# A two-layer diffusion trunk on one core: low activation halves stored backwards in one tensor with the high ones, and gate tiles that take both in one matmul of 512 columns

## What is computed

```python
h  = rms_norm(x, norm_w) * (1 + scale) + shift          # latent tokens
hc = rms_norm(ctx, norm_w) * (1 + scale_c) + shift_c    # context tokens
# SSD mixer: w_in gives z (4096), x (4096), B and C (8 groups x 128 each), dt
z, xbc, dt = jnp.split(t @ w_in, ...)
xbc = silu(conv_centred(xbc, conv_w, conv_b))           # width 5
...                                                     # chunked scans in both directions give y
y   = y * silu(z)
out = rms_norm(y, gn_w) @ w_out
```

## Time and profile before

| what | value |
|---|---|
| median of 3 runs | 2082.49 us (2082.2 to 2082.69) |
| the profiled execution, its own time | 2082.66 us |
| its span in the trace | 2081.0 us, mean granted TensorE clock 0.99 |
| TensorE busy | 2020.3 us (97% of the span), 10490 matmuls |
| TensorE weight loads | 1673.6 us (80%) |
| VectorE busy | 1459.7 us (70%) |
| ScalarE busy | 966.8 us (46%) |
| GpSimd busy | 671.5 us (32%) |
| chain that ended last | PE 80%, DVE 7%, DMA 4%, issue 3%, ACT 3%, POOL 2% |

### The profile page before, as it was taken

One profiled execution on the slowest core, in us unless ns is written; L12 is line 12 of the kernel. 1 busy time (PEld: TensorE's weight loads), 2 busy tenths in 40 slices (PEclk: granted clock), 3 DMA queues, 4 the chain that ended last, 5 costly groups with the idle time before them and its releaser, 6 DMA issues.

```text
span 2081.0 us, 31064 instructions
## 1 busy us (share of the span) xinstructions
PE 2020.3 (97%) x10490; PEld 1673.6 (80%) x10490; DVE 1459.7 (70%) x2070; ACT 966.8 (46%) x1397; POOL 671.5 (32%) x568
## 2 busy tenths in 40 slices
PE   5999999999999999999999999999999999999998
PEld 2567888888888888878878888888888888888886
DVE  5257777777777777774348887787878787877544
ACT  3244444445444444453355445445444444456443
POOL 1135666555555555635200211111112111110011
PEclk8999999999999999999999999999999999999999
DMA  9976666766666766646453554554554645456654
GB/s 352 370 218 148 165 170 176 182 173 175 165 175 172 179 175 175 165 131 174 110 151 85 153 146 127 151 136 127 150 139 123 166 116 146 132 151 197 227 184 155
DMA packets 418610, 349.23 MB, mean 168 GB/s; under 512 B 13600, under 2 KB 358272, under 8 KB 417920
## 3 DMA queue, kind: packets, MB, share of 16 engines
q1 hardware_dynamic: 393456, 273.43, 45.9%
q0 software_dynamic: 19968, 70.26, 14.1%
q10 hardware_dynamic: 5136, 4.89, 0.7%
HBM read 344.21 MB, written 4.33 MB: 167 GB/s over the span
## 4 chain that ended last, share of the span: by engine, by line
PE 80%; DVE 7%; DMA 4%; issue 3%; ACT 3%; POOL 2%; SPq 0%; DVEq 0%; POOLq 0%; ACTq 0%
PE bank L366 20%; PE bank L370 20%; PE bank L368 20%; DMA arena<-in_na_ada_w_dram 3%; PE bank L2255 3%; PE bank L2257 2%; PE bank L2256 2%; DVE w_lo L351 2%; PE bank L2193 1%; PE bank L2174 1%; DVE arena L1624 1%; PE bank L1996 1%; PE bank L1970 1%; PE bank L2188 1%; PE bank L1998 1%
## 5 line engine op out<-in xcount | busy, mean ns | idle before, releaser
L366 PE MATMUL bank<-act_hi,w_hi 128*128 128x512 f32 (+1 forms) x2448 | 906.7, 370 | 18.0 <-DVE w_lo L351 10.6
L370 PE MATMUL bank<-act_hi,w_lo 128*128 128x512 f32 (+1 forms) x2448 | 889.1, 363 | 0.0
L368 PE MATMUL bank<-act_lo,w_hi 128*128 128x512 f32 (+1 forms) x2448 | 888.8, 363 | 0.0
L351 DVE TENSOR_TENSOR w_lo<-arena,w_hi 128x2048 fp32r<-128x2048 f32 x184 | 435.6, 2368 | 210.1 <-ACT w_hi L347 147.7
L366 PEld LDWEIGHTS bank<-act_hi,w_hi 128*128 128x128 f32 x2448 | 463.0, 189 | 104.4 <-DVE w_lo L351 19.9
L370 PEld LDWEIGHTS bank<-act_hi,w_lo 128*128 128x128 f32 x2448 | 462.9, 189 | 73.7
L368 PEld LDWEIGHTS bank<-act_lo,w_hi 128*128 128x128 f32 x2448 | 463.5, 189 | 68.1
L610 POOL TENSOR_TENSOR acc<-acc,arena 128x512 f32<-128x512 f32 x224 | 330.4, 1475 | 122.9 <-ACT arena L835 113.6
L347 ACT ACTIVATE w_hi<-arena 128x2048 fp32r<-128x2048 f32 x138 | 263.8, 1911 | 85.2 <-PE bank L2257 78.2
L835 ACT ACTIVATE arena<-arena,cond_c 128x512 f32<-128x512 f32 x256 | 171.3, 720 | 264.6 <-POOL acc L610 152.5
L1392 DVE SCALAR_TENSOR_TENSOR arena<-arena,cond_c 128x512 f32<-128x512 f32 x240 | 248.4, 1035 | 65.3 <-DMA arena<-in_ssd_ada_w_dram 39.2
(11 more groups left out here) (255 smaller groups left out, 2166.0 us busy)
## 6 DMA issues: line engine op xcount, KB each, us to landing
arena<-in_ssd_w_in_dram SPq DMA_DIRECT2D x81, 1024.0 KB, 6.0
arena<-in_na_w_in_dram SPq DMA_DIRECT2D x58, 1024.0 KB, 7.4
arena<-in_ssd_ada_w_dram POOLq DMA_DIRECT2D x96, 512.0 KB, 4.1
arena<-in_na_ada_w_dram SPq DMA_DIRECT2D x64, 512.0 KB, 9.2
arena<-in_ssd_w_out_dram SPq DMA_DIRECT2D x32, 1024.0 KB, 5.1
arena<-in_na_ada_w_dram POOLq DMA_DIRECT2D x32, 512.0 KB, 4.2
arena<-in_na_w_out_dram SPq DMA_DIRECT2D x16, 1024.0 KB, 6.2
arena<-cs_scr SPq DMA_DIRECT2D x64, 256.0 KB, 5.2
```

The source lines that it names most:

```text
L351: nc.vector.tensor_tensor(w_lo[:, n0 % 2, :], raw[slot], w_hi[:, n0 % 2, :].bitcast(F32), ALU.subtract).then_inc(s_lo, 1)
L366: nc.tensor.matmul(bank[b][:, 0:cols], hi[:, w], act_hi3[:, k, 0:cols], start=(k == 0), stop=False)
L368: nc.tensor.matmul(bank[b][:, 0:cols], hi[:, w], act_lo3[:, k, 0:cols], start=False, stop=False)
L370: mm = nc.tensor.matmul(bank[b][:, 0:cols], lo[:, w], act_hi3[:, k, 0:cols], start=False, stop=(k == KT - 1))
```

## The change

`act_hi` and `act_lo` become one tensor `act` with 16 blocks of 1024 columns. In a block the low parts come first, in reverse order of the tokens, then the high parts in their own order, so that the middle 512 columns are: latent low parts backwards, latent high parts forwards. All writers and readers of `act_lo3` go through a view with step -1; `y_low` of the output projection is stored forwards, in the same places.

The G tiles use a new `project_z`. For each k it issues one matmul of 512 columns (`w_hi` by the middle 512 columns) and one of 256 (`w_lo` by the latent high parts, into the bank's second half); for the last k the 256-wide one comes first. The bank then holds the high x low part, backwards, in its first half and the rest in its second. The C tiles stay as they were.

VectorE gets `z_sum`: a copy of the first half read backwards into `silu_z`, a wait for it, and a sum with the second half into `silu_z`, which frees bank 0. ScalarE's tanh now reads `silu_z` and waits for that; it stands behind `hi_s(5 + 2j)` instead of ahead of it (in the last group it stays ahead of the second output tile's high part). VectorE's `z_gate_s` stands behind `lo_s(5 + 2j)`, reads only SBUF, and no longer frees the bank. In the last group `z_sum(3)` stands behind `y_low(0, 8)` and ahead of `fin_lo(1)`.

The diff, with lines left out that only carry context:

```diff
@@ -57,7 +57,7 @@
 OUT_BANK = (6, 0, 6, 0)
-SSD_STEPS = 54
+SSD_STEPS = 62
@@ -118,8 +118,7 @@
             pass
-        act_hi = sb("act_hi", [P, KT * TOK], F32R)
-        act_lo = sb("act_lo", [P, KT * TOK], F32R)
+        act = sb("act", [P, KT * 2 * TOK], F32R)
         w_hi = sb("w_hi", [P, 2, D], F32R)
@@ -159,12 +158,17 @@
-        act_hi3 = act_hi[:, :].rearrange("p (k t) -> p k t", k=KT)
-        act_lo3 = act_lo[:, :].rearrange("p (k t) -> p k t", k=KT)
-        def y_place(act3, k):
-            return act3[:, k, LAT:TOK] if k < KT else act3[:, k - KT, 0:LAT]
+        act3 = act[:, :].rearrange("p (k t) -> p k t", k=KT)
+        act_hi3 = act3[:, :, TOK:2 * TOK]
+        act_lo3 = act3[:, :, 0:TOK][:, :, ::-1]
+        def y_hi(k):
+            return act3[:, k, TOK + LAT:2 * TOK] if k < KT else act3[:, k - KT, TOK:TOK + LAT]
+        def y_lo(k):
+            return act3[:, k, 0:CTX] if k < KT else act3[:, k - KT, CTX:TOK]
@@ -373,6 +377,21 @@
                 mm.then_inc(s_used, 1)
+        def project_z(pe, n0, turn):
+            b = n0 % 2
+            pe.wait_ge(s_lo, turn.at(n0 + 1))
+            pe.wait_ge(s_free[b], turn.half(n0 // 2))
+            for k in range(KT):
+                w = slice(k * P, (k + 1) * P)
+                if k == KT - 1:
+                    nc.tensor.matmul(bank[b][:, LAT:TOK], w_lo[:, b, w], act_hi3[:, k, 0:LAT], start=False, stop=False)
+                mm = nc.tensor.matmul(bank[b][:, :], w_hi[:, b, w], act3[:, k, CTX:CTX + 2 * LAT],
+                                      start=(k == 0), stop=(k == KT - 1))
+                if k < KT - 1:
+                    nc.tensor.matmul(bank[b][:, LAT:TOK], w_lo[:, b, w], act_hi3[:, k, 0:LAT], start=False, stop=False)
+            mm.then_inc(s_used, 1)
@@ -1027,8 +1046,8 @@
             def z_tanh_s(j, t10):
-                act.wait_ge(s_used, t10.at(N_SSD + 3 + 2 * j + 1))
-                nc.scalar.activation(z_tanh, bank[0][:, 0:LAT], ACT.Tanh, scale=0.5).then_inc(s_zth, 1)
+                act.wait_ge(s_free[0], t10.half((N_SSD + 3 + 2 * j) // 2 + 1))
+                nc.scalar.activation(z_tanh, silu_z[j % 2], ACT.Tanh, scale=0.5).then_inc(s_zth, 1)
@@ -1070,7 +1089,7 @@
                     act.wait_ge(s_y, k + 1)
-                    nc.scalar.activation(y_place(act_hi3, k), y_t[:, k, :], ACT.Copy,
+                    nc.scalar.activation(y_hi(k), y_t[:, k, :], ACT.Copy,
                                          scale=colk[:, V_GN + k:V_GN + k + 1]).then_inc(s_yhi, 1)
@@ -1105,8 +1124,8 @@
                 else:
+                    hi_s(1, t10)
                     z_tanh_s(3, Turn(g, 10, -10))
-                    hi_s(1, t10)
                     decays(-1, t4)
@@ -1142,8 +1161,8 @@
                     if j < PAIRS - 1:
+                        hi_s(5 + 2 * j, t10)
                         z_tanh_s(j, t10)
-                        hi_s(5 + 2 * j, t10)
                         if j == 0:
@@ -1632,10 +1651,17 @@
+            def z_sum(j, t10):
+                dve.wait_ge(s_used, t10.at(N_SSD + 3 + 2 * j + 1))
+                step(nc.vector.tensor_copy(silu_z[j % 2], bank[0][:, 0:LAT][:, ::-1]))
+                step.wait()
+                nc.vector.tensor_tensor(silu_z[j % 2], silu_z[j % 2], bank[0][:, LAT:TOK], ALU.add)\
+                  .then_inc(s_free[0], 1)
             def z_gate_s(j, t10, t4):
                 dve.wait_ge(s_zth, t4.at(j + 1))
-                nc.vector.scalar_tensor_tensor(silu_z[j % 2], z_tanh, 1.0, bank[0][:, 0:LAT], ALU.add,
-                                               ALU.mult).then_inc(s_free[0], 1)
+                dve.wait_ge(s_free[0], t10.half((N_SSD + 3 + 2 * j) // 2 + 1))
+                step(nc.vector.scalar_tensor_tensor(silu_z[j % 2], z_tanh, 1.0, silu_z[j % 2], ALU.add, ALU.mult))
@@ -1762,8 +1788,8 @@
                     nc.vector.scalar_tensor_tensor(
-                        y_place(act_lo3, k), y_t[:, k, :], colk[:, V_GN + k:V_GN + k + 1],
-                        y_place(act_hi3, k).bitcast(F32), ALU.mult, ALU.subtract).then_inc(s_ylo, 1)
+                        y_lo(k), y_t[:, k, :], colk[:, V_GN + k:V_GN + k + 1],
+                        y_hi(k).bitcast(F32), ALU.mult, ALU.subtract).then_inc(s_ylo, 1)
@@ -1774,8 +1800,9 @@
                 else:
+                    z_sum(3, Turn(g, 10, -10))
+                    lo_s(1, t10)
                     z_gate_s(3, Turn(g, 10, -10), Turn(g, 4, -4))
-                    lo_s(1, t10)
                     combine(-2, t4)
@@ -1809,6 +1836,7 @@
                         y_low(0, 8)
+                        z_sum(3, t10)
                         fin_lo(1)
@@ -1816,7 +1844,7 @@
                     if j < PAIRS - 1:
-                        z_gate_s(j, t10, t4)
+                        z_sum(j, t10)
                         if first and j == 0:
@@ -1826,6 +1854,7 @@
                         lo_s(5 + 2 * j, t10)
+                        z_gate_s(j, t10, t4)
                         if j == 0:
@@ -2229,7 +2258,7 @@
                         states(j - 1, t4, t1.at(1))
-                    project(pe, N_SSD + 3 + 2 * j, t10, cols=LAT)
+                    project_z(pe, N_SSD + 3 + 2 * j, t10)
                     if j == 0:
@@ -2251,7 +2280,7 @@
                     w = slice(512 * kk, 512 * kk + 512)
-                    hi, lo = y_place(act_hi3, k)[:, tok], y_place(act_lo3, k)[:, tok]
+                    hi, lo = y_hi(k)[:, tok], y_lo(k)[:, tok]
                     nc.tensor.matmul(b[:, :], hi, w_hi[:, n % 2, w], start=(k == 0), stop=False)
```

## The result

| | us |
|---|---|
| before, median of 6 runs | 2082.34 (2079.46 to 2085.09) |
| after, median of 6 runs | 2091.59 (2089.45 to 2092.83) |
| ratio, 95% interval | 1.0046 [1.0036, 1.0057] |
| forecast | 2084.2, range 2080.5 to 2088.5 |

The change makes the kernel slower by 9 us, more than twice the 4.2 us that can be told from nothing. It is outside the range, on the side of the first rival, which had a chance of 0.12. The profiled execution after took 2092.83 us (span 2091.2).

What follows compares the result with a forecast made beforehand. The chain through VectorE, ScalarE and GpSimd was taken to bound the SSD groups, despite TensorE's 97% busy share. First group +0.4, middle groups +0.6, last group +0.7, backward access 0: +1.7 us, giving 2084.2, range 2080.5 to 2088.5.

Steps and rivals of the forecast that it cites:

- first rival: At every high x low matmul (L368): a backward read on TensorE is dear, 2484 us at half pace; chance 0.12.
- Backward access: Low operand of every projection but the gates': reading it backwards taken to cost 0, with 400 us the far end.
- rule that spoke against the change in pair 0: VectorE with two SBUF inputs and GpSimd reading SBUF exclude each other; `z_gate_s` meets GpSimd's masks, slack covers it.
- What bounds the kernel: SSD groups: TensorE is 97% busy, but the chain through VectorE, ScalarE and GpSimd is already longer, 20.4 against 19.94 us.
- What the gate tiles save: 32 gate tiles: each goes from 5.76 to 5.55 us, 0.21 saved; 6.8 us if nothing else ended later.
- The link: VectorE, ScalarE and GpSimd, from one L707 to the next: 0.34 - 0.26 = 0.08 us longer, `z_sum` hidden.
- B's wait: Next group's B tile waiting for its low weights, two links later: a new wait of about 0.6 us in each group.
- Middle groups: Six middle SSD groups: each costs 0.1 us instead of saving 0.84, +0.6 us in all.
- First group: First SSD group: X2 already waits 1.65 us, so no gate saving counts and the chain lengthens; +0.4 us.
- Last group and output: X2 and X3 gain 0.4 us; second output tile's split waits for `z_sum`, third tile about 1.1 late; +0.7 us.
- second rival: ScalarE's high split does not move up, so each link costs 0.34 us; 2087.4 us; chance 0.11.
- the third: Low weights of X2, X3 and B follow a faster TensorE, so 24 gate tiles save 5.1 us; 2078.5 us; chance 0.08.

Runs made afterwards that it cites:

- two-piece kernel: The changed kernel with low parts forwards, the gate's wide operand two forward 256-column pieces in one matmul; 2082.65 us, ratio 1.0010 against the kernel before.

## Why the prediction was wrong, and where it was right

**The step that failed is "Backward access", where "I take 0".** A 512-wide backward read on TensorE costs 6.1 ns, 2.7% of a step of 0.227 us. I bounded it by 400 us above and 0 below, named 1.3 ns a matmul as the point from which that rival decides, and then took the near end by an analogy from VectorE's reads of PSUM. Those say nothing of TensorE's reads of SBUF. The runs with only the direction changed show 0.39 us more in each head in its place, and 4.5 us in the whole. The exclusion of a gain was wrong in part too: 256-wide tiles gained 5.6 ns per block of three. The rule of the Trainium skill ("SBUF — State Buffer", the section on the DMA port swizzle), from which the prediction concluded that backward float32 is free, doesn't give that price: for this operand the runs with only the direction changed decide against the conclusion.

Where the time goes, from the profiled executions, which are 10.2 us apart (the medians 9.25): 4.5 us ahead of the head shown, 2.6 from there to the attention output, 0.96 in the attention output, -1.1 in a stretch ahead of the first group, and 0.55 + 1.26 - 0.14 + 1.54 = 3.2 from the first group on. The 2.6 and 0.96 are the direction's: they are 2.5 and 0.95 with the direction alone. Of the 4.5 some 3 are, if the heads ahead pay 0.39 each as well, which is an estimate: the first projection tile starts at 155.2 to 161.0 us in the fourteen profiled executions, and the first heads vary as well, with DMA waits. The -1.1 is for the most part the clock. In that stretch (49.80 us before, 48.66 after) TensorE sits idle for some 3 us, and its next steps are 0.43 us apart at a granted clock of 0.50, the lower of its two levels, 1.2 GHz: 14 such steps before and 9 after, so the mean granted clock is 0.90 before and 0.93 after. The other kernels with the new gate tiles or `z_sum` have 8 to 11 of them, the rest 9 to 14; whether the change has a part in it isn't shown.

By medians the direction alone costs 4.5 us and the change with a free direction 1.6, together 6.0 of 9.25. The interval of each of the three is about 2 us to either side, so these runs don't tell whether the other 3.2 come of the two acting together. In the middle groups they do, by some 0.6 of their 1.26 us.

The rule that spoke against the change in pair 0 ("SBUF: two separate sides", on the same page of the Trainium skill) does hold here. Timeline of the kernel after, GpSimd's masks and `z_gate_s` in pair 0:

```profile
1348.00 2.57 POOL L715 TENSOR_SCALAR_AFFINE_SELECT arena<-arena 128x256 f32<-128x256 f32 x4 [25.02 <-ACT arena L1170]
1349.01 0.62 DVE L1664 SCALAR_TENSOR_TENSOR arena<-arena 128x256 f32<-128x256 f32 x1
```

It takes 0.62 us beside the masks, in seven of the eight groups, and 0.42 in the other pairs. In the middle groups no tile behind it waits (X2 and X3 start without one), so the 0.2 us are covered, as was said.

Step by step:

- *What bounds the kernel.* Right for the middle groups: links are bound by the chain, and three runs say so. The wide gate matmul undone, nothing changes; one VectorE operation taken out, 2.26 us go; the saving on TensorE turns up as idle time.
- *What the gate tiles save.* The sign was right, the size wrong: 0.353 us a pair, not 0.347, so 0.10 us a tile, not 0.21. Of the pair the wide step takes 0.236 us (mean of 448 steps), not the 0.227 of a 512-wide tile. No run separates why; it isn't the direction. In the middle groups it costs nothing, since the saving is worth nothing there. (32 times 0.21 is 6.7 and 24 times 5.0, not the 6.8 and 5.1 of the prediction; nothing hangs on it.)
- *The link.* L707 to L707 was 20.41 us, forecast at 20.5, and took 20.47. `z_sum` is hidden, as forecast.
- *X1's wait* rose from 0.32 to 0.41, not 0.53, in line with a gate tile's saving of 0.10 rather than 0.21. *B's wait* is 0.23 rather than 0.6, for the same reason and since backward X tiles make TensorE later; in the two-piece kernel it is 0.34.
- *Middle groups.* +0.6 forecast; +0.38 with a free direction, +1.26 as changed. The forecast's 0.1 a group was loose: its own figures, 1397.70 against 1397.67, give 0.03. The other 0.9 comes with the direction. That the direction alone costs 0.29 there fits, since in that run the gate tiles gain by it; that it is the backward X and B tiles is argued, not shown.
- *First group* +0.4 forecast, +0.44 and +0.55 measured.
- *Last group and output.* +0.7 forecast; +1.3 in the two-piece kernel, +1.4 after. The mechanism held row by row; the third output tile came 1.3 us late, and two tiles on the lag had grown to 1.55. The cost was 0.6 too small: the gain ahead of the output was 0.3 (0.14 as changed) and not 0.4, the third tile came 1.3 late and not 1.1, and I stopped adding at it.
- *L368's pace*, named as the sign that would prove me wrong, did: a block of three takes 0.6876 us in the heads, against 0.6815.

What stays open: the gate's product on another engine than VectorE, which the run without it (2.26 us in six groups) points to, wasn't tried.

The second rival (the high split does not move up) is out by the rows above: it starts ahead of the tanh. So is the third (the chain is not the bound), by the same three runs.

## What to carry to other kernels

An operand that two thousand matmuls read must have its price per matmul from a row of TensorE itself; 1.3 ns was enough to decide here, and the analogy was not that fine. A trick that saves TensorE time is worth nothing where TensorE already waits for a chain on other engines: follow that chain first, since taking out one 0.42 us operation per pair there was worth 2.26 us in six groups, and shortening their 24 gate tiles nothing. When an operation on an in-order engine gets a new predecessor, follow its queue until the lag has stopped growing, and where independent work can stand ahead of it, put it there.

## What the runs showed of the hardware that I had not expected

- **Direction of the moving operand.** In 512-wide fp32r matmuls it costs 6.1 ns, the same for each of the three products (50.82 against 49.64 us a head), and about as much at sixteen other start places (50.93 against 50.52). In 256-wide ones a block of three gets shorter, 0.3538 against 0.3594 us. Why they differ in sign isn't settled.
- **16 bytes.** Moving the split weights, and all that lies behind them, by 16 bytes costs 1.13 us a head and 3.7 us in the output stage, 2113.38 us in all against 2079.96 before; 512 bytes don't. It is seen both where the weights are loaded and where they are streamed. With 128 bytes a head took 50.52 us and the output stage 187.49, but there the low parts were staggered too. Since all that lies behind moved with the weights, which tensor minds isn't shown, nor the multiple that is needed. For studies like this one it is a trap: an experiment that makes a tensor a little longer measures the move as well.
- **The two look alike.** All three products backwards, and everything forwards with the weights moved by 16 bytes, give nearly the same blocks of three: 0.7001 and 0.6998 us at 512 columns (0.6815 before), 0.3549 and 0.3550 at 256 (0.3594 before). Whether one mechanism is behind both is open.
